# Seven chunks in place of six in block 2's split products, with GpSimd making part of the low parts

## What is computed

```
h = rms_norm_2(x, norm_mix) * (1.0 + sc_m) + sh_m
proj = h @ w_in                      # 256 x 1024 times 1024 x 6400
xr, gr, dq, dk, dv, sq, sk, sv, gl = jnp.split(proj, offsets, axis=-1)
...
gates = sigmoid(gl).reshape(B, S, 3, D)
merged = einsum('bsnd,bsnd->bsd', gates, branch_proj)
x = x + g_m * (merged @ w_out)
x = x + g_f * moe_ffn(rms_norm_2(x, norm_ffn) * (1.0 + sc_f) + sh_f, ...)
```

## Time and profile before

| | |
|---|---|
| median of 3 runs | 2579.81 us (2578.34 to 2582.88) |
| the profiled execution's own time | 2580.93 us |
| its span, first to last instruction | 2579.2 us |
| PE busy over the span | 2551.8 us, 99% |
| DVE, ACT, POOL busy | 1378.3, 835.3, 78.4 us |
| mean granted TensorE clock | 0.999 |

### The profile page before, as it was taken

The page is one execution under the profiler, slowest core; times in us unless marked ns, Lnnn a source line. Parts: engine busy times, 40 slices in busy tenths (PEclk is TensorE's granted clock), DMA queues, the critical chain, the costliest instruction groups (busy, mean ns, idle before and its releaser), DMA issues.

```text
span 2579.2 us, 36169 instructions
## 1 busy us (share of the span) xinstructions
PE 2551.8 (99%) x14173; PEld 1800.0 (70%) x14173; DVE 1378.3 (53%) x1777; ACT 835.3 (32%) x1363; POOL 78.4 (3%) x103
## 2 busy tenths in 40 slices
PE   9999999999999999999999999999999999999998
PEld 6889898888888998998889988833333333333333
DVE  7966785698798668748945684222121121112112
ACT  4514441454354245324524362121121121121111
POOL 0000200000000020000001000000000000000000
PEclk9999999999999999999999999999999999999999
DMA  7785343467666833445564545799999999999998
GB/s 231 228 287 176 134 148 147 144 194 232 221 199 212 297 131 131 143 166 166 186 205 143 201 161 209 309 401 427 426 428 428 427 428 428 427 427 428 428 427 359
DMA packets 265915, 702.23 MB, mean 272 GB/s; under 512 B 14404, under 2 KB 156816, under 8 KB 216528
## 3 DMA queue, kind: packets, MB, share of 16 engines
q1 hardware_dynamic: 250992, 650.03, 65.8%
q0 software_dynamic: 12496, 46.90, 5.1%
q10 hardware_dynamic: 2320, 3.83, 0.4%
HBM read 696.47 MB, written 6.60 MB: 273 GB/s over the span
## 4 chain that ended last, share of the span: by engine, by line
PE 85%; DMA 10%; SPq 3%; DVE 1%; ACT 1%; issue 0%; DVEq 0%; ACTq 0%
PE acc L2037 12%; PE acc L2052 6%; PE acc L1200 6%; PE mix L1203 6%; PE acc L1201 6%; PE acc L1302 5%; PE acc L1318 4%; PE acc L1133 3%; PE acc L1252 2%; PE acc L1772 2%; PE acc L1564 2%; PE acc L1150 2%; DMA ring<-in_w 2%; PE mix L2022 2%; PE acc L1260 2%; PE acc L1258 2%
## 5 line engine op out<-in xcount | busy, mean ns | idle before, releaser
L2739 DVE TENSOR_TENSOR ring_parts<-ring,area_parts 128x1536 fp32r<-128x1536 f32 (+1 forms) x181 | 290.9, 1607 | 63.1 <-ACT area_parts L2224 19.4
L3621 DVE COPY zz<-acc 128x512 f32<-128x512 f32 x32 | 22.1, 691 | 525.4 <-PE acc L2037 525.4
L1200 PE MATMUL acc<-area_parts,branch_parts 128*128 128x512 f32 x672 | 266.6, 397 | 2.0 <-DVE big_parts L2739 2.0
L1203 PE MATMUL mix<-zz_parts,big_parts 128*128 128x512 f32 x672 | 262.2, 390 | 0.0
L1201 PE MATMUL acc<-ring_parts,area_parts 128*128 128x512 f32 x672 | 262.0, 390 | 0.0
L2224 ACT ACTIVATE area_parts<-ring 128x1536 fp32r<-128x1536 f32 (+1 forms) x126 | 168.8, 1342 | 146.2 <-PE mix L1203 101.5
L2843 DVE SCALAR_TENSOR_TENSOR zz_parts<-area_parts,ring_parts 128x1536 fp32r<-128x1536 f32 (+1 forms) x126 | 199.2, 1581 | 9.4
L1200 PEld LDWEIGHTS acc<-area_parts,branch_parts 128*128 128x128 f32 x672 | 126.2, 188 | 28.7 <-DVE big_parts L2739 3.6
L1203 PEld LDWEIGHTS mix<-zz_parts,big_parts 128*128 128x128 f32 x672 | 126.2, 188 | 27.2
L1201 PEld LDWEIGHTS acc<-ring_parts,area_parts 128*128 128x128 f32 x672 | 126.4, 188 | 25.0
L2215 ACT ACTIVATE area<-acc 128x512 f32<-128x512 f32 (+1 forms) x67 | 32.0, 478 | 341.7 <-PE acc L1966 331.6
(11 more groups left out here) (600 smaller groups left out, 4941.8 us busy)
## 6 DMA issues: line engine op xcount, KB each, us to landing
big<-in_w SPq DMA_DIRECT2D x77, 1024.0 KB, 25.5
ring<-in_w SPq DMA_DIRECT2D x76, 1024.0 KB, 25.7
ring<-in_w_in SPq DMA_DIRECT2D x72, 1024.0 KB, 7.0
area<-in_w SPq DMA_DIRECT2D x58, 1024.0 KB, 25.5
ring<-in_ffn_up SPq DMA_DIRECT2D x86, 640.0 KB, 5.6
spare<-in_w SPq DMA_DIRECT2D x38, 1024.0 KB, 25.7
ring<-in_ffn_up SPq DMA_DIRECT2D x86, 384.0 KB, 4.3
area<-in_w_ada POOLq DMA_DIRECT2D x24, 1024.0 KB, 7.5
```

The source lines that it names most:

```text
L1200: pe.matmul(abank(a, b), xg[:, k, half(b)], wg[:, k, :], start=k == 0, stop=False, skip_group_check=True)
L1203: mm = pe.matmul(kbank(a, b), xk[:, k, half(b)], wk[:, k, :], start=k == 0, stop=k == SPLIT - 1, skip_group_check=True)
L2739: return v.tensor_tensor(out, a, b, op)
```

## The change

`SPLIT_2` becomes 7, so one more chunk of every half is split and one stays float32. In units 3, 4, 6, 7 and 8 the subtraction that makes the low part is shared: DVE does chunks 0 to 4, POOL chunks 5 and 6 (`low_part2`), and DVE waits for `low_made` ahead of the difference. In units 2 and 5 DVE does all seven. POOL's pieces stand between its transfers. `lruw` moves, since the parts grow: one half of it goes to the end of `big`, the other to the end of `spare`. A semaphore is renamed to make room for the new one.

```diff
-SPLIT_2 = 6
+SPLIT_2 = 7
+OWN_2 = 5
+SHARED_2 = (3, 4, 6, 7, 8)
...
-        pools = [[flat(big[:, 28:32, :], "c t"), 0, 4 * T]]
-        lruw = carve(2, 4, P)
+        lruw = [shaped(m, (4, P)) for m in (flat(big[:, 30:32, :], "c t"), spare[:, 2 * WU - 4 * P:2 * WU])]
...
+        low_made = sem("last_lower_parts_by_gpsimd")
+        lru_sq = silu_ready
...
             def lower2(n, b):
                 l, g = half_unit2(n, b, ring_parts), wg2[:, b].bitcast(F32)
+                own = slice(0, OWN_2 if n in SHARED_2 else SPLIT_2)
                 v.wait_ge(g_ready, half_parts2(n, b))
-                tt(l, half_unit2(n, b, ring), g, ALU.subtract)
+                tt(l[:, own], half_unit2(n, b, ring)[:, own], g[:, own], ALU.subtract)
                 v.drain()
+                if n in SHARED_2:
+                    v.wait_ge(low_made, low_parts2(n, b))
                 v.scalar_tensor_tensor(out=wk2[:, b], in0=g, scalar=-1.0 / STEP, in1=l.bitcast(F32), op0=ALU.mult, op1=ALU.add) \
                     .then_inc(k_ready, 1)
...
-            g.memset(lruw, 0.0)
+            for m in lruw:
+                g.memset(m, 0.0)
...
+            def low_part2(n):
+
+                ks = slice(OWN_2, SPLIT_2)
+                for b in range(2):
+                    g.wait_ge(g_ready, half_parts2(n, b))
+                    g.tensor_tensor(half_unit2(n, b, ring_parts)[:, ks], half_unit2(n, b, ring)[:, ks],
+                                    wg2[:, b, ks].bitcast(F32), ALU.subtract).then_inc(low_made, 1)
 
             g.wait_ge(tab_ready, 2)
             g.dma_start(io["scr1"][0:HEADS, :], tab[0:HEADS, 0, :]).then_inc(scr_a, 16)
             g.dma_start(io["scr1"][HEADS:12, :], tab[HEADS:12, 1, :]).then_inc(scr_a, 16)
+            low_part2(3)
             g.wait_ge(scr_a, 32)
...
                         bass.AP(io["scr1"].tensor, 0, [(U, 12), (0, P), (1, U)])).then_inc(scr_b, 16)
+            low_part2(4)
             g.wait_ge(scr_b, 16)
...
+            for n in SHARED_2[2:]:
+                low_part2(n)
```

More of the change, by code:

```diff
@@ L522, in mixed_blocks @@
         lru_m = rows_ready
-        lru_sq = sem("lru_sq")
+        low_made = sem("last_lower_parts_by_gpsimd")
+        lru_sq = silu_ready
         lru_out = sem("lru_out")
@@ L816, in last_group2, with low_parts2 @@
             return n if n < 2 else half_group2(n, 1) if n < GATE2 + 3 else G_GATE2 + 3 + n - GATE2
+        def low_parts2(n, b):
+            return 0 + 2 * SHARED_2.index(n) + b + 1
         def half_place2(n, b):
@@ L1664, in n_lru @@
                     for c in range(4):
-                        mm = pe.matmul(c2(mix, 4 * g + c), lruw[:, g, c, :], xc[:, c, :], start=True, stop=True)
+                        mm = pe.matmul(c2(mix, 4 * g + c), lruw[g][:, c, :], xc[:, c, :], start=True, stop=True)
                 mm.then_inc(lru_gates, 1)
@@ L3503, in _ @@
             swa_probs(score0[:, 2:4, :], 0, P).then_inc(z0_prob, 1)
-            v.wait_ge(lru_sq, 1)
+            v.wait_ge(lru_sq, 24 * LAYERS + 1)
             tt(lb, lb, lt, ALU.mult)
@@ L3769, in _ @@
                     for c in range(4):
-                        g.dma_start(lruw[lo:lo + 64, n, c, lo:lo + 64], w[two, :, c, :]).then_inc(lru_landed, 16)
+                        g.dma_start(lruw[n][lo:lo + 64, c, lo:lo + 64], w[two, :, c, :]).then_inc(lru_landed, 16)
+            def low_part2(n):
[4 more added lines that the diff above has]
+                                    wg2[:, b, ks].bitcast(F32), ALU.subtract).then_inc(low_made, 1)
             g.wait_ge(tab_ready, 2)
```

## The result

The changed kernel takes 2587.98 us (median of 8 runs, 2585.24 to 2589.79), the kernel before 2579.35 (2577.95 to 2584.02): ratio 1.0031, interval 1.0022 to 1.0039, 8.6 us slower. The profiled execution has a span of 2587.7 us against 2579.2.

The account below looks back on a forecast made before the run. PE was taken to pace the split stage; waits +4.85 and PE's saving -2.11 gave +2.7 us, the queue +0.5: +3.2 on 2579.81, so 2583.0 us. Range, 8 in 10: 2577.5 to 2587.0.

Parts of the forecast that it names:

- The rest of the sum: Split stage without the queue: PE's waits +4.85 us with PE's saving of 2.11, giving +2.7 us.
- PE's gain: Each of 14 halves drops 4 float32 records for 6 short matmuls: 0.15 us less a half, -2.11 us.
- The chain and the turns: Load, ACT, DVE and POOL turns delay PE in units 3, 4, 5, 6 and 8: +4.85 us net.
- POOL's piece: POOL's part of the subtraction takes turns with DVE's: a shared half costs 1.07 us more, 6.67.
- The queue's term: bias_blocks and bias_diff, delayed behind POOL's pieces, slow loads: 0.5 us in unit 4, 1.2 in unit 5; +0.5 in all.
- The third rival: POOL's transfers land on the loads of units 4 to 6: +5.7 us, 2585.5 us; chance 0.14.
- its own sign: The third rival decides once units 4 and 6 together wait 2.5 us more than in the forecast's sum.
- Unit 6: PE's wait at this unit's first half: 2.92 us lost without the queue, 2.22 with it, in place of 0.63.
- Passing to the end 1:1: A shift of the split stage reaches the kernel's end in full; the later stages keep their length.

Follow-up runs that it names:

- e10: The changed kernel, unaltered, profiled and timed once more: 2587.14 us.
- e9: e1 run once more, unaltered, for one profiled execution: 2582.23 us.
- e6: e5 with bias_swa read only after unit 6 has landed: median 2577.21 us, 2.8 below the kernel before, ratio 0.9991.
- e7: The kernel before, with six chunks, given both edits of e6: median 2579.75 us, 0.3 below the kernel before.
- e1: The changed kernel with POOL's bias transfers ahead of its pieces, every share kept: median 2582.66 us, 2.65 above the kernel before, ratio 1.0007.
- e3: The changed kernel with all seven chunks made by DVE, nothing on POOL: median 2582.53 us, 2.5 above the kernel before.
- e4: The kernel before with unit 5's load issued one half later: median 2586.27 us, 6.3 above the kernel before.
- e2: The kernel before, POOL holding bias_blocks and bias_diff until the upper parts of units 3's and 4's second halves: median 2582.38 us, 2.4 above.
- e5: e3 with PE doing a half's upper-part products before waiting for DVE: median 2577.78 us against 2580.04 for the kernel before.
- e11: e1 with e5's order on PE: median 2578.51 us against 2580.20 for the kernel before.

## Why the prediction was wrong

Forecast: +3.2 us, 2577.5 to 2587.0, within 0.2% at 0.82. Measured: +8.6, slower by 0.31%. The direction was right, and the size and the chances were wrong. Two terms failed. The transfers on POOL's queue were put at +0.5 us and measured 2.1 to 3.0; the clock, at nothing, measured 1.5 to 2.6. The traces give this. The change's stage is 8.8 us longer, of which 2.6 are clock (e10: 6.7, of which 1.5), and e9's, without collision or fall, is 3.2 longer: 8.8 - 2.6 - 3.2 = 3.0, and for e10 6.74 - 1.5 - 3.16 = 2.1. The rest of the sum, +2.7, stands against e9's 3.2.

- **PE's gain** of 0.15 us a half was right: 5.84 measured for 5.85. e6 against e7 shows it in units 2 to 5, and 1.3 of the 2.1 us over the stage.
- **The chain and the turns** were right where they stood alone: 0.56 and 1.23 forecast for units 3 and 4, 0.53 and 1.23 measured; 0.62 for unit 8, 0.73 measured; 1.07 for POOL's piece, 1.10 measured (1.18 less the drain's 0.08). That last match has some luck in it: a piece that runs alone takes 1.27 to 1.30 and not the 1.04 of the earlier trace rows, but behind DVE's 1.49 it ends 1.15 later. Prices of 1.49, 1.70 and 2.03 us were met to the hundredth. e1, where the queue is in order, gives +2.65 for the +2.7 of the sum without the queue, closer than its interval (-0.5 to +4.1) can tell; some of its executions may hold a fall of the clock.
- **The queue's term failed.** "I take 0.5 in unit 4 and 1.2 in unit 5", +0.5 us in all, bounded by "at the most 2.7 for the blocks, 0.6 for the 512 KB". ACT began on unit 5 5.8 us later than before, and PE lost 5.2 us there besides the clock, where the sum had 0.85. The bound came from an HBM-to-SBUF read of 1024 KB beside a load (1.2 us) and went by KB. `bias_blocks` goes from HBM to HBM and took 14.8 us here, 7 of them beside unit 5's load; the length of this overlap would have been a bound that holds. Also, I laid part of the blocks on unit 4's load. In the change that load lost nothing (ACT 7.72 us behind unit 3's start, 7.80 before). The third rival had the right mechanism at 0.14, and at +5.7 it was nearer than the forecast. But it laid the waits on units 4 and 6 (2.93 and 4.32 us, 0.04 for unit 5), and by its own sign, 2.5 us more than the sum in those two together, it did not come true: they lost 1.23 + 0.79 + 0.73.
- **The clock was not in the sum at all.** A wait of 2.92 us (4.32 in the third rival) was forecast and costed at its length. Behind waits of 3.0 to 4.8 us the runs show a loss of another 1.4 to 2.6 us at 1.2 GHz in five of six traces; the wait of 2.42 in e3 cost only itself. Without the clock the stage of the first trace would be 6.2 us longer than before.
- **Unit 6** was to lose 2.22 with the queue (2.92 without) and lost 0.73. Unit 5's wait came first, and the load of unit 6 was then early. That is the trade named in the text ("what unit 5 waits more, unit 6 waits less"), and it worked.
- **Passing to the end 1:1** held: stage +8.8, median +8.6; in e3 +2.63 and +2.52; in e4 +6.13 and +6.26. In e1 and e2 stage and median part by over 2.5 us, as said above.

## What to carry to other kernels

When work is put into a queue that also issues transfers, list each transfer behind it with its new issue time, and lay its whole duration, not its bytes alone, over the loads it now meets. Where PE is 99% busy, a late load costs its delay, and here in five of six traces with a wait of 3 us or more also a stretch at half clock. Before an engine is given a share of a chain, look for cover: reordering PE so that it uses the parts in the order in which they are made shortened the stage by 4.1 us from e3 to e5 (the medians by 4.8), where the share on POOL brought nothing (e1 against e3) or cost 0.7 of the stage (e11 against e5).

## What the runs showed of the hardware

- The 2304 KB of `bias_blocks` from HBM to HBM landed in 11.4 to 12.5 us in the ten traces where they went out near unit 2's start, and in 13.9 to 16.4 in the three (the change, e2, e10) where they went out 14 to 17 us later and lay beside unit 5's 2 MB load. ACT's start on that unit moved from 7.9 us behind unit 4's start to between 12.6 and 13.7.
- Behind idle times of PE of 2.99, 3.19, 3.19 (behind 1.59), 4.62 and 4.80 us the granted clock was 0.50 for a time; behind 2.42 and one of 3.09 it stayed 1.00. The same kernel (e1 and e9) did both. In e2 the first seven short matmuls behind the wait were still spaced by 0.12, and the fall came 0.9 us behind its end. The stretch at half clock differed: 2.6 us lost in two traces, 1.4 to 1.5 in three.
- POOL and DVE, both with two operands in SBUF, take turns by whole instructions: when DVE is first, its 1.49 and then 1.18 us until POOL's piece is done and the difference starts; when POOL is first, 2.43 for DVE's 1.49. The Trainium skill says so in SBUF — State Buffer, "SBUF: two separate sides" (an exclusive lock for two-input DVE operations against a POOL operation that reads SBUF); the traces agree.
